# Output products of the second block: weight tiles of 512 columns over four input chunks

## The reference

```python
h = swiglu(rms_norm_2(x, ng[0]), ffn_w_gate[l, 0], ffn_w_up[l, 0], ffn_w_down[l, 0])
x = x + 0.5 * rms_norm_2(h, ng[1])
h = rms_norm_2(x, ng[2])
...                                  # l == 0: rwkv7_mix and retention_mix; l == 1: sparse attention and short conv
h = jnp.concatenate([y_a, y_b], axis=-1) @ ev_w_out[i]
...
def swiglu(x, w_gate, w_up, w_down):
    return (jax.nn.silu(x @ w_gate) * (x @ w_up)) @ w_down
```

## Time and profile before

| | |
|---|---|
| Median of 3 runs | 3389.76 us (3383.2 to 3390.05) |
| The profiled execution | 3388.8 us, its span 3387.0 us |
| TensorE | matmuls busy 2871.2 us (85%), 17440; weight loads busy 2257.7 us (67%) |
| VectorE | 2461.5 us (73%) |
| ScalarE | 771.0 us (23%) |
| GpSimd | 636.4 us (19%) |
| DMA | 868.23 MB, mean 256 GB/s |

### The profile page before, as it was taken

The page is one execution under the profiler, slowest core; times in us unless marked ns, Lnnn a source line. Parts: engine busy times, 40 slices in busy tenths (PEclk is TensorE's granted clock), DMA queues, the critical chain, the costliest instruction groups (busy, mean ns, idle before and its releaser), DMA issues. The chain is left out here.

```text
span 3387.0 us, 44524 instructions
## 1 busy us (share of the span) xinstructions
PE 2871.2 (85%) x17440; PEld 2257.7 (67%) x17440; DVE 2461.5 (73%) x4664; ACT 771.0 (23%) x1994; POOL 636.4 (19%) x520
## 2 busy tenths in 40 slices
PE   8999977777776988777777779998768999998898
PEld 8889843333332988433333329997767999997798
DVE  7455677777777976677777878777456878767786
ACT  4223221222221433222222221012313001023300
POOL 0000044444454000444444440000000000000000
PEclk9999998888988999888888889998879999999899
DMA  6454599999999544999999995654014666652364
GB/s 208 145 172 151 177 418 420 412 417 404 406 412 397 183 139 159 418 419 412 414 408 397 417 395 168 203 168 132 15 32 141 184 203 183 196 176 93 122 193 143
DMA packets 470274, 868.23 MB, mean 256 GB/s; under 512 B 18865, under 2 KB 398641, under 8 KB 402353
## 3 DMA queue, kind: packets, MB, share of 16 engines
q0 software_dynamic: 73728, 536.90, 38.4%
q1 hardware_dynamic: 396048, 328.24, 30.5%
q10 hardware_dynamic: 288, 0.24, 0.0%
HBM read 855.89 MB, written 9.44 MB: 255 GB/s over the span
## 5 line engine op out<-in xcount | busy, mean ns | idle before, releaser
L2733 PE MATMUL banks<-arena,arena 128*128 128x512 f32 x1744 | 916.9, 684 | 325.6 <-ACT arena L2808 325.1
L2733 PEld LDWEIGHTS banks<-arena,arena 128*128 128x128 f32 x1744 | 372.1, 220 | 852.2 <-issue 453.8
L2691 POOL DMA_INDIRECT arena<-in_peer_uv,arena x512 | 631.4, 1233 | 1316.6 <-PE banks L2733 654.9
L2966 DVE CUSTOM_DVE_ANT_0 arena<-arena,normed 128x1024 f32<-128x1024 f32 x512 | 625.5, 1222 | 247.2 <-DMA arena<-in_peer_uv,arena 245.0
L445 DVE TENSOR_TENSOR weight_ring_part<-weight_ring,weight_high_parts 128x2048 fp32r<-128x2048 f32 (+2 forms) x244 | 539.9, 2213 | 8.3
L3523 PE MATMUL banks<-normed_columns_part,weight_high_parts 128*128 128x256 f32 x1408 | 395.3, 281 | 3.0 <-DVE weight_ring_part L445 2.4
L3524 PE MATMUL banks<-normed_part,weight_high_parts 128*128 128x256 f32 x1408 | 393.3, 279 | 0.0
L3525 PE MATMUL banks<-normed_columns_part,weight_ring_part 128*128 128x256 f32 x1408 | 393.1, 279 | 0.0
L844 PE MATMUL banks<-weight_high_parts,arena_part 128*128 128x256 f32 x1216 | 345.0, 284 | 44.3 <-DVE weight_ring_part L445 26.1
L442 DVE CAST weight_high_parts<-weight_ring 128x2048 fp32r<-128x2048 f32 (+2 forms) x244 | 289.7, 1187 | 94.8 <-PE banks L846 74.5
L846 PE MATMUL banks<-weight_high_parts,arena_part 128*128 128x256 f32 x1216 | 342.1, 281 | 0.0
(11 more groups left out here) (583 smaller groups left out, 4256.7 us busy)
## 6 DMA issues: line engine op xcount, KB each, us to landing
weight_ring<-in_ffn_w_gate SPq DMA_DIRECT2D x88, 512.0 KB, 3.7
weight_ring<-in_ffn_w_up SPq DMA_DIRECT2D x88, 512.0 KB, 4.8
weight_ring<-in_ev_w_in SPq DMA_DIRECT2D x33, 1024.0 KB, 5.4
weight_ring<-in_ffn_w_down SPq DMA_DIRECT2D x32, 1024.0 KB, 5.2
weight_ring<-in_od_w_in SPq DMA_DIRECT2D x23, 1024.0 KB, 5.3
weight_ring<-in_xa_wkv SPq DMA_DIRECT2D x16, 1024.0 KB, 5.3
weight_ring<-in_peer_wq SPq DMA_DIRECT2D x16, 1024.0 KB, 15.6
weight_ring<-in_ev_w_out SPq DMA_DIRECT2D x12, 1024.0 KB, 5.5
```

The source lines that it names most:

```text
L2691: pool.indirect_dma_start(out=ring[:, slot(i, s), :], out_offset=None, in_=table, in_offset=bass.IndirectOffsetOnAxis(ap=index[:, i % 2, s ...
L2733: mm = pe.matmul(k.ps[:, 2 * b + half, :], diag[:, g % 2, s, :], v, start=n == b * PEER_TOPK, stop=n == last_mixed[b])
L2966: dve.tensor_tensor_reduce(out=ring[:, here, 0:D], in0=ring[:, here, 0:D], in1=k.xn[:, i % NB, :], scale=1.0, scalar=0.0, op0=ALU.mult, op ...
```

## The change

In `land` with a norm behind it, a block has 512 columns and a tile four chunks (`HALF`), so a matmul is 512 wide and a result fills a whole bank of 512 float32. The plan gets its tiles from a new function, for `ffn_w_down_2`, `xa_wo_2`, `ev_w_out_2` and `od_w_out_2`. `tiles` is 2, `per` is 6 for a feed-forward (five tiles of four chunks, 1 MB, and one of two, 0.5 MB), 2 for a mixer and 1 for a cross-attention (1 MB). VectorE's multiplication by the gain and ScalarE's squaring take 512 columns at once, four of each instead of eight; their results lie where they did. Everything behind (scaling, transposes, next inputs) goes on in pieces of 256 columns. Side products use the banks from 0, once two results have been read. Cut to its core:

```diff
 def land(...):
-        per = -(-kc // KC)
-        tiles = D // WIDTH
+        wide = post is not None
+        deep, width = (HALF, 2 * WIDTH) if wide else (KC, WIDTH)
+        per = -(-kc // deep)
+        tiles, pieces = D // width, D // WIDTH
...
         def bank(j, b):
-            return self.ps[:, (j * NB + b) % depth, 0:WIDTH]
+            return self.ps[:, (j * NB + b) % depth, 0:width]
...
+        share = width // WIDTH
+        spots = 2 * D // (2 * width)
+        side_at = 0 if wide else LATE_BANK
+        ahead_of_side = side_at + SIDE_BANKS
...
-                                k = t * KC + c
+                                k = t * deep + c
...
-                            if n >= 4:
-                                act.wait_ge(self.squared.sem, self.squared.start + n - 3)
-                            act.activation(self.dump[:, n % 4 * WIDTH:(n % 4 + 1) * WIDTH], bank(j, b), ACT.Square,
+                            if n >= spots:
+                                act.wait_ge(self.squared.sem, self.squared.start + n - spots + 1)
+                            act.activation(self.dump[:, n % spots * width:(n % spots + 1) * width], bank(j, b), ACT.Square,
...
-                                dve.tensor_tensor(weighted[:, j * NB + b, :], bank(j, b), self.gain[:, j * WIDTH:(j + 1) * WIDTH],
-                                                  ALU.mult).then_inc(self.tile_out.sem, 1)
+                                dve.tensor_tensor(weighted[:, share * j:share * (j + 1), b, :], pieces_of(bank(j, b)),
+                                                  pieces_of(self.gain[:, j * width:(j + 1) * width]), ALU.mult).then_inc(self.tile_out.sem, 1)
...
+def wide_tiles(w):
+    rows = w.shape[0] // P
+    return [[w[k * P:min(k + HALF, rows) * P, c:c + 2 * WIDTH].rearrange("(c p) n -> p c n", p=P)]
+            for c in range(0, D, 2 * WIDTH) for k in range(0, rows, HALF)]
...
-        add_streamed(tiles_of(ins["ffn_w_down_2"][l, i], 0, D))
+        add_streamed(wide_tiles(ins["ffn_w_down_2"][l, i]))
```

More of the change, by code:

```diff
@@ L791, in bank, with pieces_of @@
         def bank(j, b):
[L792 removed]
+            return self.ps[:, (j * NB + b) % depth, 0:width]
         def piece(src, j, b):
             return src[:, b, j * WIDTH:(j + 1) * WIDTH]
[L796 removed]
+        weighted = self.xn[:, :, :].rearrange("p b (h d) -> p (b h) d", d=WIDTH).rearrange("p (j b) d -> p j b d", b=NB)
+        def pieces_of(ap):
+            return ap.rearrange("p (i d) -> p i d", d=WIDTH)
+        share = width // WIDTH
+        spots = 2 * D // (2 * width)
+        side_at = 0 if wide else LATE_BANK
+        ahead_of_side = side_at + SIDE_BANKS
         with self.step(hold=nxt is not None) as block:
@@ L817, in beside @@
                             pe.wait_ge(self.memory_in.sem, memory_loaded)
-                            pe.wait_ge(self.tile_out.sem, self.tile_out.start + LATE_BANK + SIDE_BANKS)
-                            pe.wait_ge(self.squared.sem, self.squared.start + LATE_BANK + SIDE_BANKS)
-                        self.multiply_side(pe, u0 + first, u0 + last, bank_at=LATE_BANK)
+                            pe.wait_ge(self.tile_out.sem, self.tile_out.start + ahead_of_side)
+                            pe.wait_ge(self.squared.sem, self.squared.start + ahead_of_side)
+                        self.multiply_side(pe, u0 + first, u0 + last, bank_at=side_at)
                 ahead = 1 if per > 1 else 0
@@ L849, in _ @@
                 beside(ahead, 3)
-                for j in range(tiles - 1 if post is None else 0, tiles if nxt is not None else 0):
+                for j in range(pieces - 1 if post is None else 0, pieces if nxt is not None else 0):
                     pe.wait_ge(self.landed.sem, self.landed.start + (j + 1) * NB)
@@ L885, in _ @@
                             act.wait_ge(self.tile_out.sem, self.tile_out.start + n + 1)
-                            if n >= 4:
-                                act.wait_ge(self.squared.sem, self.squared.start + n - 3)
-                            act.activation(self.dump[:, n % 4 * WIDTH:(n % 4 + 1) * WIDTH], bank(j, b), ACT.Square,
-                                           accum_out=self.out_parts[:, b * 4 + j:b * 4 + j + 1]).then_inc(self.squared.sem, 1)
+                            if n >= spots:
+                                act.wait_ge(self.squared.sem, self.squared.start + n - spots + 1)
+                            act.activation(self.dump[:, n % spots * width:(n % spots + 1) * width], bank(j, b), ACT.Square,
+                                           accum_out=self.out_parts[:, b * tiles + j:b * tiles + j + 1]).then_inc(self.squared.sem, 1)
                     act.wait_ge(self.out_ready.sem, self.out_ready.start + 1)
                     act.activation(self.out_root, self.out_mean, ACT.Sqrt).then_inc(self.out_rooted.sem, 1)
-                    for j in range(tiles if nxt is not None else 0):
+                    for j in range(pieces if nxt is not None else 0):
                         self.keep_high(act, j, nxt, high_out)
                         if j == 1 and fill is not None:
-                            self.keep_side(act, sides, bank_at=LATE_BANK)
+                            self.keep_side(act, sides, bank_at=side_at)
             @block.vector
@@ L923, in _ @@
                 dve.wait_ge(self.squared.sem, self.squared.start + tiles * NB)
-                dve.tensor_reduce(self.sums, self.out_parts.rearrange("p (b j) -> p b j", b=NB), AX.X, ALU.add).then_inc(done.sem, 1)
+                dve.tensor_reduce(self.sums, self.out_parts[:, 0:NB * tiles].rearrange("p (b j) -> p b j", b=NB), AX.X, ALU.add).then_inc(done.sem, 1)
                 if unscaled:
@@ L941, in _ @@
                 dve.wait_ge(self.tile_out.sem, self.tile_out.start + tiles * NB)
-                for j in range(tiles):
+                for j in range(pieces):
                     for b in range(NB):
-                        dve.scalar_tensor_tensor(piece(self.x, j, b), weighted[:, j * NB + b, :], self.out_scale[:, b:b + 1],
+                        dve.scalar_tensor_tensor(piece(self.x, j, b), weighted[:, j, b, :], self.out_scale[:, b:b + 1],
                                                  piece(self.x, j, b), ALU.mult, ALU.add).then_inc(self.landed.sem, 1)
@@ L950, in _ @@
                 if nxt is not None:
-                    dve.wait_ge(self.landed.sem, self.landed.start + tiles * NB)
-                    self.keep_low(dve, tiles - 1, nxt, high_out, low_out)
-            self.landed.adds(NB * tiles)
+                    dve.wait_ge(self.landed.sem, self.landed.start + pieces * NB)
+                    self.keep_low(dve, pieces - 1, nxt, high_out, low_out)
+            self.landed.adds(NB * pieces)
             self.squared.adds(NB * tiles)
@@ L1366, in weight_order @@
     add_whole(memory_tiles_2(ins, 0)[LATE:])
-    add_streamed(tiles_of(ins["ev_w_out_2"][0], 0, D))
+    add_streamed(wide_tiles(ins["ev_w_out_2"][0]))
     attention_2(0)
@@ L1373, in weight_order @@
     add(tiles_of(w, DSA_IN, 1992))
-    add_streamed(tiles_of(ins["od_w_out_2"][0], 0, D))
+    add_streamed(wide_tiles(ins["od_w_out_2"][0]))
     attention_2(1)
```

3 lines of the change are left out of this document (1 added, 2 removed).

## The result

The changed kernel takes 3397.37 us (median of 10 runs, 3392.99 to 3406.07) against 3387.49 us for the kernel before (10 runs beside it, 3379.31 to 3393.91): ratio 1.0034, 95% interval 1.0025 to 1.0042. By the ratio it is slower by 11.5 us (the two medians differ by 9.9), where a gain of 16.8 us had been forecast (3373.0 from 3389.8); the time lies above the range. The profiled execution took 3401.55 us, its span is 3399.8 us.

The account below looks back on a forecast made before the run. TensorE's matmul distance was taken to bound six of eight stretches; in the two cross-attentions TensorE waits. 3388.8 - 17.3 + 3.6 + 3.6 - 4.8 - 1.7 = 3372.2 us profiled, median 3373.0 us; range 3364 to 3387.

Parts of the forecast that it names:

- Part 1: All eight products: 2 x 1344 matmuls become 1344 wide ones at 216 ns, together saving 17.3 us.
- The forecast's 216 ns: Distance assumed between 512-wide float32r matmuls, from rows with the same array time and the same load.
- a wide pace above 220 ns: Distance between 512-wide matmuls in the changed kernel's profile that would show the forecast wrong.
- The upper bound of 235.6: Bound in ns on a 512-wide matmul, 2 x 117.8, if all of today's excess is per column.
- rival A: No gain in the stream: excess belongs to columns, a wide matmul costs two narrow ones; 3391 us, chance 0.12.
- Rival C: Kernel slower, nearly all for a pace between 234 and 245, up to 3412; chance 0.05.
- part 5: Cross-attention products: sum of squares 4.8 us earlier in the first, longer split ahead included, and 1.7 us in the second.
- Part 2: Middle of each feed-forward: TensorE waits 0.9 us for VectorE's split, 3.6 us in all; bounds 0.8 to 1.2.
- Part 3: End of six stages: longer last read, multiplication and squaring add 0.6 us each, 3.6 us; bounds 0.4 to 0.8.
- Part 4: Cross-attention ahead of the product: second tile's split before the first head's maximum takes 3.47 instead of 1.85, + 1.6 us.
- Rival B: Half clock after waits in cross-attentions and feed-forwards costs 1.6 us each, six times 9.6, so 3382.6 us; chance 0.13.

Follow-up runs that it names:

- the streams: Kernels without the model, only runs of matmuls, with widths, types and operand starts varied: float32r 512 wide 226.7 to 233.4 ns, bfloat16 512 wide 215.8 ns.
- the balanced cut: Changed kernel with a feed-forward's 22 chunks cut 4, 4, 4, 4, 3, 3: 3393.41 us, ratio 1.0010; with input tiles also moved 48 elements: 3385.64 us.

## Why the prediction was wrong

**Part 1, the stream, is the step that failed.** The forecast's 216 ns are the distance between plain float32 matmuls of 256 columns, (3.62 - 0.38) / 15. That a float32r matmul of 512 columns goes at their pace, and that the excess of today's 256-wide one is a load that isn't hidden, were my estimates, and no run shows either: at full clock it took 226.7 to 233.4 ns in the runs, and in the streams the excess is still there at 512 columns. Those rows say what a plain float32 matmul takes, not what a float32r one costs above its columns. In the changed kernel it is 233.3 ns, 17.3 ns more; over 1344 matmuls that is 23.3 us, and the miss of the median is 24.4. That these are so near is partly chance, as other terms were off in both directions (below). The sign that the prediction named for this, a wide pace above 220 ns, is there.

The two shorter counts in that sum, 84 pairs in the even mixer and 256 in a feed-forward, leave out what stands at the low clock, on the estimate that nothing is saved there. That much the traces show: at a granted clock of 0.50 the even mixer's narrow matmuls are 213 ns apart (20 distances from 2522.46 to 2526.72, before) and the wide ones 427 ns (10 from 2527.16 to 2531.43, after). The low clock takes in the first 24 narrow matmuls of that product, and the first 16 or so of the third feed-forward's.

The stream was to save 17.3 us. Between the two profiles its own distances come out even (first feed-forward + 1.6 us, the slow-paced third one - 2.2), and about 3 us of that draw are not the change's. The third and the last feed-forward of the kernel before have 3.4 us each at the lower clock level at their start (clock 0.97; 0.55 over their first 3.47 us), the changed kernel has none; at full clock the stream costs about 3 us more than before.

The upper bound of 235.6 was right. That a pair at 117.8 ns came to 235.6, near what was measured, reads like a sign afterwards, and I priced rival A, which reads it so, at 0.12. A's outcome, a wide matmul for two narrow ones, is near the truth. Its premise, that the excess is per column, is not what the streams show: with both operands at the same start it is 13.3 ns at 512, 384 and 256 columns, and at the kernel's difference of 48 it is 20.0 ns for the wide one and 6.7 or 11.1 for a narrow one.

**Rival C's turning point** of 234 ns, 18 ns above 216, was worked out for a loss that a measurement can tell (16.8 us of gain and 6.8 us of loss over 1344 matmuls): the sum there is 3373.0 + 24 = 3397 us, not the "3380 + 18" of the text. At 233.3 ns the forecast's other terms give 3373.0 + 23.3 = 3396.3, 6.5 us slower than 3389.8. Measured are 11.5 (8.5 to 14.2), so those terms were too good by some 5 us, most of it in part 5. (The forecast's own sum, 3372.2 + 1.0, is 3373.2; nothing hangs on the 0.2.)

**Part 2, the stall**: predicted 0.9 us each, measured 1.08, inside the bounds of 0.8 to 1.2, at the predicted place and in all four. The size is partly luck: the short tile covers 2.8 us and not 2.59, which leaves 0.67, and 0.4 us pass between the end of the fifth tile's use, the split and TensorE's restart, for which only the upper bound had room.

**Part 3, the tail**: 0.6 us, exact (1.28 to 1.88), and so is the 0.11 in it that was an estimate: the last result is read 0.43 us behind the last start (2231.97 to 2232.40) where it was 0.32. I counted six; in the three feed-forwards that carry side units it costs next to nothing, as TensorE goes from the last side unit straight to the transposes (at 2235.68, 3.7 us behind the start of the last matmul; before at 2233.44, 3.6 us behind it). So 1.8 us and not 3.6.

**Part 4**: + 1.6 us, exact, twice.

**Part 5, the attentions**: the gain of 4.8 us in the first one became about 0.6: TensorE's path from the product's start to the transposes is 2.2 us less, and 1.6 went ahead of it. I had followed VectorE's queue to the sum of squares and not TensorE's beyond it, where three side units stand, and had missed the wait of the empty call ahead of the last tile. In the second, 2.5 us were won in the product, 1.6 given back ahead, and 0.9 to the clock: nothing is left of the 1.7.

**Rival B, the clock**: its mechanism is there in the attentions and not in the middle of the feed-forwards. The lengthened wait ahead of the heads' products is followed by low clock in seven of twelve cases over six profiles, at 0.9 to 1.1 us each, not 1.6. In the pair of profiles it is one of the two. The waits of 1.08 us in the four feed-forwards are followed by none, nor is that of 2.10 us between starts in the first attention's product (the stretch stands above with 1.00). The products' stretches above stand at 1.00 or at what the earlier trace rows have.

**The sum by the measured terms** for this pair of profiles: stream 0, stall 4.3, tail 1.8, attentions - 0.6 and 0: 5.5 us. The spans differ by 12.8. Of the rest, 4.8 us stand where the change does nothing, in the four first halves of the feed-forwards. The sums of their windows, before and after:

```profile
sum 497.77, PE 493.91; mean PE 123.48
```
```profile
sum 502.59, PE 498.99; mean PE 124.75
```

They are 1056 narrow matmuls each, and their pace stands at 113.3 or at 117.8 ns, which differs from stage to stage and from one profile to the next in either kernel (126.4, 126.2, 122.4 and 122.8 us before; 125.3, 124.1, 126.2 and 127.0 after). The way from the first feed-forward's product to the even mixer's is 2.8 us longer, again without a part in the change. The other way, the kernel before loses 2 times 1.1 us right ahead of the two products with low clock. TensorE's rows at the start of its second and its third feed-forward's product:

```profile
2737.01 0.36 PE L844 MATMUL banks<-weight_high_parts,arena_part 128*128 128x256 f32 x1 [1.57 <-PEq L385]
2932.93 0.36 PE L844 MATMUL banks<-weight_high_parts,arena_part 128*128 128x256 f32 x1 [2.67 <-PEq L385]
```

The twelve profiles of a whole kernel have one or the other of these two waits at each such start, 1.6 us or 2.6 to 2.7; the changed kernel has the short one four times. Of the 28 short ones none has low clock in the first microseconds of the product, of the 20 long ones 17 have. What makes the wait long was not found, and whether it brings the low clock was not tested. So a balance drawn from a single pair of profiles is not good to 1 us.

With the products' own narrow pairs at 113.3 throughout, the change would cost 9 us more in the stream than a draw, 14.5 in all; with the paces of this profile, at full clock, 8.5. The measured 11.5 lies between. What decides between the two narrow paces wasn't found; the fourth combination of the streams at 48 shows that both can be had without any kernel around them. Nor was it settled why the balanced cut gives 8 us, twice, where the waits come to 4.3.

## What to carry to other kernels

Before an engine's pace is borrowed for a new shape, ask whether the row has the same type of operand; for float32r it decided the sign here, and a stream of sixty matmuls of the new shape, with the operands where the kernel has them, would have settled it. A faster unit of work that comes with coarser tiles pays for them in fixed places: a short last tile that no longer covers a split, a longer step in front of a serial chain, a wait that is written in numbers of results. When a change alters a tile's shape, its place in SBUF is a parameter of its own, to be tried with both kernels, and with an eye on what else the moved tile serves. And before two profiles are subtracted, look whether the stretches that the change leaves alone agree: here they differ by as much as the terms in question.

## What the runs showed of the hardware

- A column takes 0.417 ns at full clock, by the steps from 256 to 384 and 512. A float32r matmul costs 6.7 to 20 ns above its columns (226.7 to 233.4 ns for 512, 173.3 for 384 in one place, 113.3 to 120.0 for 256), a bfloat16 one 2.5 ns (215.8 and 109.2). VectorE at work beside it changes nothing (226.7).
- The excess goes by the distance between the starts of the moving and the stationary operand modulo 64 elements of 4 bytes: 512 wide 227.1, 228.8, 232.5, 233.4 ns at 0, 16, 32 and 48; 256 wide 119.8, 117.8, 118.5 and 113.4 (or 117.8).
- 192 bytes of it over the eight products, and two narrow ones of the first block, are worth - 7.8 us in the changed kernel (1.0034 to 1.0011) and + 11 us in the kernel before (1.0032).
- Behind waits of 2.34 us TensorE's granted clock was at half (0.50 to 0.51) for 3.4 us in seven of twelve places; at the start of a feed-forward's product, behind waits of 2.6 to 2.7 us, in 17 of 20, and behind waits of 1.6 us in none of 28.
- That stretch of low clock costs 0.9 to 1.1 us in an attention (9.6 us become 10.5 to 10.8).
